# Latent attention with keys on partitions: three buffers for the rounded operands, value products in pairs, inverses by small transfers

## What is computed

```
s = (einsum('bhqd,bhkd->bhqk', q_nope, k_nope)
     + einsum('bhqr,bkr->bhqk', q_pe, k_pe)).astype(float32) * scale
p = softmax(s, axis=-1)
out = einsum('bhqk,bhkd->bhqd', p, v)
```

## Time and profile before

| | |
|---|---|
| median of three runs | 3343.63 us |
| profiled execution's own time | 3337.21 us |
| its span | 3335.4 us |
| TensorE matmuls busy | 3153.4 us (95%) |
| VectorE busy | 2228.0 us (67%) |
| ScalarE busy | 1356.4 us (41%) |
| mean granted TensorE clock | 0.976 of full |
| first and last exponential of the stage | 1970.2 and 2548.8 us from the span's start |

### The profile page before, as it was taken

One profiled execution on the slowest core, in us unless ns is written; L12 is line 12 of the kernel. 1 busy time (PEld: TensorE's weight loads), 2 busy tenths in 40 slices (PEclk: granted clock), 3 DMA queues, 4 the chain that ended last, 5 costly groups with the idle time before them and its releaser, 6 DMA issues. The chain is left out here.

```text
span 3335.4 us, 42351 instructions
## 1 busy us (share of the span) xinstructions
PE 3153.4 (95%) x16250; PEld 2516.4 (75%) x16250; DVE 2228.0 (67%) x2448; ACT 1356.4 (41%) x2259; POOL 571.6 (17%) x587
## 2 busy tenths in 40 slices
PE   7999899899999999999998989999999999999997
PEld 5888777788999999888886854444445878888875
DVE  4999666546755565778544347776776676667877
ACT  5121456465332333445674223333333433333444
POOL 0000000120222222332131100000000223332323
PEclk9999999899999999999999989999999999999998
DMA  6224685532212212667527523222221222222665
GB/s 213 70 95 150 207 262 202 173 113 73 75 61 76 70 61 70 233 216 239 176 81 287 173 69 63 56 56 56 65 55 52 100 64 84 87 83 76 236 209 196
DMA packets 302456, 415.52 MB, mean 125 GB/s; under 512 B 108840, under 2 KB 206824, under 8 KB 301232
## 3 DMA queue, kind: packets, MB, share of 16 engines
q1 hardware_dynamic: 288880, 363.12, 35.4%
q0 software_dynamic: 13376, 49.69, 4.0%
HBM read 318.49 MB, written 94.13 MB: 124 GB/s over the span
## 5 line engine op out<-in xcount | busy, mean ns | idle before, releaser
L4615 ACT ACTIVATE mla_e<-mla_scores 128x512 f32<-128x512 f32 x320 | 191.1, 597 | 391.0 <-PE mla_scores L90 383.3
L2160 DVE TENSOR_TENSOR ring_lo<-raw_rows,ring_hi 128x512 fp32r<-128x512 f32 x200 | 181.0, 905 | 202.3 <-ACT ring_hi L2011 202.0
L1283 PE MATMUL banks<-y_hi,ring_hi 128*128 128x384 f32 (+2 forms) x688 | 222.0, 323 | 4.2 <-DVEq L2148 3.7
L1285 PE MATMUL banks<-y_hi,ring_lo 128*128 128x384 f32 (+2 forms) x688 | 221.9, 322 | 0.0
L1284 PE MATMUL banks<-y_lo,ring_hi 128*128 128x384 f32 (+2 forms) x688 | 221.8, 322 | 0.0
L4645 DVE TENSOR_REDUCE mla_least<-mla_rounded 128x1 f32<-128x1024 f32 x128 | 153.1, 1214 | 86.6 <-PE mla_rounded L4534 86.4
L1283 PE MATMUL banks<-differences,ring_hi 128*128 128x512 f32 (+2 forms) x560 | 192.0, 343 | 3.4 <-ACT sums L2021 2.6
L1285 PE MATMUL banks<-differences,ring_lo 128*128 128x512 f32 (+2 forms) x560 | 191.8, 342 | 0.0
L1284 PE MATMUL banks<-differences,ring_hi 128*128 128x512 f32 (+2 forms) x560 | 191.8, 342 | 0.0
L862 DVE SCALAR_TENSOR_TENSOR ab_work<-ab_work,ab_taps 128x1295 f32<-128x1295 f32 x120 | 188.0, 1567 | 3.3
L4565 PE MATMUL mla_out<-mla_e,ckv 128*64 128x512 f32 x640 | 180.8, 645 | 0.0
(11 more groups left out here) (552 smaller groups left out, 8710.5 us busy)
## 6 DMA issues: line engine op xcount, KB each, us to landing
raw_rows<-in_ffn_w_up SPq DMA_DIRECT2D x88, 512.0 KB, 3.5
da_ada_w<-in_ada_w SPq DMA_DIRECT2D x10, 4096.0 KB, 14.5
raw_rows<-in_ffn_w_down SPq DMA_DIRECT2D x110, 256.0 KB, 3.1
raw_rows<-in_ffn_w_down SPq DMA_DIRECT2D x44, 512.0 KB, 4.7
out_raw<-scratch_act SPq DMA_DIRECT2D x66, 256.0 KB, 3.5
sums<-scratch_act SPq DMA_DIRECT2D x55, 256.0 KB, 3.4
ab_raw<-in_ab_w_in SPq DMA_DIRECT2D x20, 512.0 KB, 4.0
scratch_act<-conv_lines SPq DMA_DIRECT2D x20, 512.0 KB, 4.8
```

Of the source, the lines that this page charges most:

```text
L1283: pe.matmul(out, w_hi[:, w], b_hi[:, a:a + n], start=start and k == 0, stop=False, skip_group_check=True)
L1285: mm = pe.matmul(out, w_lo[:, w], b_hi[:, a:a + n], start=False, stop=k == KD // 2 - 1, skip_group_check=True)
L2160: dve.tensor_tensor(blocks(begun.lo(r)), source(r), blocks(begun.hi(r)).bitcast(F32), ALU.subtract)\
L4615: act.activation(e[:, tile % E_SLOTS, c * BANK:(c + 1) * BANK], s_ps[:, score_fill(h, i) % 3, :], ACT.Exp)\
```

## The change

- The rounded queries and keys get a third buffer (`q_hi`, `k_hi`, by h % 3); the rests keep two. SP loads the rounded parts of head h + 2 and the rests and values of head h + 1 at the start of head h. The pieces of the next head stand earlier (`piece_at`), the first behind block 0.
- The value products stand in pairs of key tiles, behind blocks 5, 9, 13 and 17, and the last pair behind block 1 of the next head. The sum stands behind block 5.
- VectorE adds all ten key tiles (nine adds), so the sum is one group of matmuls. There is one accumulator instead of two.
- ScalarE copies the sums to SBUF (`copy_sum`), SP turns them into a tile of 128 x 8 by eight transfers, VectorE takes the inverse of that, SP stores it to memory in one transfer and reads it back in two, spread over 64 partitions each. The last head keeps the old way.
- The rows of ones and zeros come from small tiles, by seven transfers, and the first loads of the stage come in another order.

The core of the diff (VectorE's order is in the rows above):

```diff
-    SUM_AT = 5
+    SUM_AT = 6
...
-    ADDS = KT - 2
+    ADDS = KT - 1
...
-    piece_at = {2: 0, 4: 1, 5: 2, 7: 3, 8: 4, 10: 5, 11: 6, 13: 7, 14: 8, 15: 9}
+    piece_at = {0: 0, 1: 1, 2: 2, 4: 3, 6: 4, 7: 5, 9: 6, 10: 7, 12: 8, 13: 9}
...
+        q_hi = q_first[0], sb("q_hi1", [HD + 1, SEQ], F32R), sb("q_hi2", [HD + 1, SEQ], F32R)
+        k_hi = k_first[0], sb("k_hi1", [HD + 1, T], F32R), sb("k_hi2", [HD + 1, T], F32R)
+        q_lo, k_lo = (q_first[1], sb("q_lo1", [HD + 1, SEQ], F32R)), (k_first[1], sb("k_lo1", [HD + 1, T], F32R))
...
+            def rounded(h):
+                if h >= 3:
+                    sp.wait_ge(s.s_full.sem, 2 * KT * (h - 2))
+                load_part(sp, h, q_hi[h % 3], k_hi[h % 3], q_parts[0], k_parts[0], hi_in[h % 3].sem)
+
+            def rests(h):
                 if h >= 2:
                     sp.wait_ge(s.s_full.sem, 2 * KT * (h - 1))
-                for part, signal in ((0, hi_in), (1, lo_in)):
-                    load_part(sp, h, part, qs[h % 2][part], ks[h % 2][part], q_parts, k_parts, signal[h % 2].sem)
+                load_part(sp, h, q_lo[h % 2], k_lo[h % 2], q_parts[1], k_parts[1], lo_in[h % 2].sem)
...
+            def sums_to_columns(h):
+                sp.wait_ge(s.sum_copied.sem, h + 1)
+                for t in range(XT):
+                    c, j = divmod(t, XT // 2)
+                    sp.dma_start(sum_cols[:, t:t + 1], sum_rows[c * C_V:c * C_V + 1, j * P:(j + 1) * P],
+                                 allow_slow_non_contiguous=True).then_inc(s.cols_in.sem, 16)
+
+            def store_inverses(h):
+                sp.wait_ge(s.inverted.sem, h + 1)
+                sp.dma_start(column(inv_rows[h % 2]), inv_cols[:, :], allow_slow_non_contiguous=True)\
+                  .then_inc(s.inv_stored.sem, 16)
+
+            def spread_inverses(h):
+                sp.wait_ge(s.inv_stored.sem, 16 * (h + 1))
+                sp.wait_ge(s.scaled.sem, h)
+                for c in range(2):
+                    sp.dma_start(inv[c * C_V:(c + 1) * C_V, :], row(inv_rows[h % 2, c * BANK:(c + 1) * BANK], C_V))\
+                      .then_inc(s.inv_in.sem, 16)
...
+            for n in (1, 2):
+                sp.dma_start(k_hi[n][C_NOPE:HD, :].bitcast(F32), k_parts[0][C_HEADS * C_NOPE:C_HEADS * C_NOPE + C_ROPE, :])\
+                  .then_inc(s.pe_in.sem, 16)
+            rounded(1)
+            sp.wait_ge(s.set.sem, 2)
+            for k in k_hi:
+                unit_row(k[HD:HD + 1, :], ones)
+            for k in k_lo:
+                unit_row(k[HD:HD + 1, :], zeros)
+            for q in q_lo:
+                unit_row(q[HD:HD + 1, :], zeros)
             values(0)
-            load_positions(sp, ks[1], k_parts, s.pe_in.sem)
-            head(1)
-            values(1)
             shift_row(0, 0)
             shift_row(0, 1)
+            sp.dma_start(k_lo[1][C_NOPE:HD, :].bitcast(F32), k_parts[1][C_HEADS * C_NOPE:C_HEADS * C_NOPE + C_ROPE, :])\
+              .then_inc(s.pe_in.sem, 16)
+            rests(1)
+            values(1)
+            rounded(2)
+            shift_row(1, 0)
+            shift_row(1, 1)
             for h in range(1, H):
-                if h >= 2:
-                    head(h)
-                    values(h)
-                shift_row(h, 0)
-                shift_row(h, 1)
+                if h + 1 < H:
+                    rests(h + 1)
+                    values(h + 1)
+                if h + 2 < H:
+                    rounded(h + 2)
+                sums_to_columns(h - 1)
+                store_inverses(h - 1)
+                if h + 1 < H:
+                    shift_row(h + 1, 0)
+                spread_inverses(h - 1)
+                if h + 1 < H:
+                    shift_row(h + 1, 1)
...
-                    tokens = slice(c * BANK, (c + 1) * BANK)
-                    pe.matmul(s_ps[c * C_V:(c + 1) * C_V, f % 3, :], ones[:, :], acc[:, h % 2, tokens],
-                              start=True, stop=False)
-                for c in range(2):
-                    tokens = slice(c * BANK, (c + 1) * BANK)
-                    mm = pe.matmul(s_ps[c * C_V:(c + 1) * C_V, f % 3, :], ones[:, :],
-                                   e[:, (h * KT + KT - 1) % E_SLOTS, tokens], start=False, stop=True)
+                    mm = pe.matmul(s_ps[c * C_V:(c + 1) * C_V, f % 3, :], ones[:, :], acc[:, c * BANK:(c + 1) * BANK],
+                                   start=True, stop=True)
                 mm.then_inc(s.sum_full.sem, 1)
...
                     if i == 1 and h:
+                        product(h - 1, KT - 2)
                         product(h - 1, KT - 1)
-                    if i >= 3 and i % 2:
+                    if i >= 5 and i % 4 == 1:
+                        product(h, (i - 5) // 2)
                         product(h, (i - 3) // 2)
                     if i == SUM_AT - 1 and h:
                         total(h - 1)
...
+            def copy_sum(h):
+                act.wait_ge(s.sum_full.sem, h + 1)
+                if h:
+                    act.wait_ge(s.cols_in.sem, 16 * XT * h)
+                act.activation(sum_rows[:, :], s_ps[:, sum_fill(h) % 3, :], ACT.Copy).then_inc(s.sum_copied.sem, 1)
...
-                    if i == 1 and h:
+                    if i == 2 and h:
                         copy_out(h - 1)
-                    if i == 9 and h and h % 2 == 0:
+                    if i == 6 and h:
+                        copy_sum(h - 1)
+                    if i == 18 and h and h % 2 == 0:
                         round_out(h // 2 - 1)
...
-                dve.wait_ge(s.sum_full.sem, h + 1)
-                dve.wait_ge(s.scaled.sem, h)
-                dve.reciprocal(inv, s_ps[:, sum_fill(h) % 3, :]).then_inc(s.inverted.sem, 1)
+                dve.wait_ge(s.cols_in.sem, 16 * XT * (h + 1))
+                if h:
+                    dve.wait_ge(s.inv_stored.sem, 16 * h)
+                dve.reciprocal(inv_cols[:, :], sum_cols[:, :]).then_inc(s.inverted.sem, 1)
+
+            def last_inverse():
+                dve.wait_ge(s.sum_full.sem, H)
+                dve.wait_ge(s.scaled.sem, H - 1)
+                dve.reciprocal(inv, s_ps[:, sum_fill(H - 1) % 3, :]).then_inc(s.inverted.sem, 1)
 
             def scale(h):
-                dve.wait_ge(s.inverted.sem, h + 1)
+                if h < H - 1:
+                    dve.wait_ge(s.inv_in.sem, 32 * (h + 1))
+                else:
+                    dve.wait_ge(s.inverted.sem, H)
```

More of the change, by code:

```diff
@@ L4434, in sb @@
             return ctx.enter_context(nc.sbuf_tensor(f"mla_{label}", shape, dt))
-        qs = q_first, [sb(f"q_{n}", [HD + 1, SEQ], F32R) for n in ("hi", "lo")]
-        ks = k_first, [sb(f"k_{n}", [HD + 1, T], F32R) for n in ("hi", "lo")]
+        ones = sb("ones", [P, C_V])
+        zeros = sb("zeros", [1, C_V])
+        least = sb("least", [P, 2, XT])
+        shift = sb("shift", [P, 2, XT], F32R)
+        q_hi = q_first[0], sb("q_hi1", [HD + 1, SEQ], F32R), sb("q_hi2", [HD + 1, SEQ], F32R)
+        k_hi = k_first[0], sb("k_hi1", [HD + 1, T], F32R), sb("k_hi2", [HD + 1, T], F32R)
+        q_lo, k_lo = (q_first[1], sb("q_lo1", [HD + 1, SEQ], F32R)), (k_first[1], sb("k_lo1", [HD + 1, T], F32R))
         v = v_home[:, 0, 0:2 * KT * C_V].rearrange("p (j k d) -> p j k d", j=2, k=KT)
@@ L4441, in latent_attention @@
         e = sb("e", [P, E_SLOTS, SEQ])
-        acc = sb("acc", [P, 2, SEQ])
-        ones = sb("ones", [P, C_V])
-        least = sb("least", [P, 2, XT])
-        shift = sb("shift", [P, 2, XT], F32R)
+        acc = sb("acc", [P, SEQ])
+        sum_rows = sb("sum_rows", [P, BANK])
+        sum_cols, inv_cols = sb("sum_cols", [P, XT]), sb("inv_cols", [P, XT])
         s_ps = ctx.enter_context(nc.psum_tensor("mla_scores", [P, 3, BANK], F32))
@@ new lines, in spread_inverses, with unit_row @@
+            def spread_inverses(h):
[4 more added lines that the diff above has]
+                      .then_inc(s.inv_in.sem, 16)
+            def unit_row(dst, value):
+                count = dst.shape[1] // C_V
+                sp.dma_start(dst.bitcast(F32).rearrange("p (a n) -> p a n", n=C_V),
+                             value[0:1, :].rearrange("p (a n) -> p a n", a=1).broadcast_to([1, count, C_V]))\
+                  .then_inc(s.unit_in.sem, 16)
@@ L4597, in _ @@
                         piece(h + 1, piece_at[i])
+            product(H - 1, KT - 2)
             product(H - 1, KT - 1)
@@ L4610, in exponential @@
                     act.wait_ge(s.o_step.sem, before + 1)
-                    if before % KT == KT - 1:
-                        act.wait_ge(s.sum_full.sem, before // KT + 1)
-                    else:
-                        act.wait_ge(s.added.sem, ADDS * (before // KT) + max(1, before % KT))
+                    act.wait_ge(s.added.sem, ADDS * (before // KT) + max(1, before % KT))
                 act.activation(e[:, tile % E_SLOTS, c * BANK:(c + 1) * BANK], s_ps[:, score_fill(h, i) % 3, :], ACT.Exp)\
@@ L4692, in _ @@
                 if h:
```

(31 more changed lines are left out.)

53 lines of the change are left out of this document (23 added, 30 removed).

## The result

The changed kernel took 3356.83 us (median of 6 runs, 3352.71 to 3360.73), the kernel before 3343.66 in the same session (6 runs, 3340.55 to 3346.26). The ratio is 1.004, interval 1.0027 to 1.0053: slower by 13 us, where I had put 3240 and left 0.04 for slower.

What follows compares the result with a forecast made beforehand. TensorE was taken to bound the attention stage, with holes and half clock. 14 heads from 37.16 to 30.5 us save 93.2, the start 13.4, the last head loses 2.4: 104.2 saved, forecast 3240 us, range 3220 to 3275.

Steps and rivals of the forecast that it cites:

- the walk: One attention head timed from its first score block through copy, columns, inverse, store, spread, scale and adds: 30.5 us a head.
- the spread: Reading the stored inverses back in two transfers of 128 KB: taken to land 2.5 us after issue.
- x = 2.0: Adds ending x us into the next head; beyond 2.0, a longer chain lengthens the head 1:1; x was 2.5.
- the reason for the low clock: The hole at each head's start, after which TensorE's clock was at 1.2 GHz; expected to go, leaving granted clock 1.00 mid-stage.
- the hole: TensorE's wait for the next head's rounded operands, 32.1 us over 14 heads; third buffers were to remove it.
- rival A: The transfers set the head: each leg 1 us longer, 33.5 us a head, total 3284; chance 0.12.
- Rival C: Slower than before: columns 7.2 and spread 3.0 us later in queues, 49 us slower, 3392; chance 0.04.
- threshold of 7 us of extra chain: In rival C, the extra chain per head from which the kernel turns slower: 104 / 15 = 7 us.
- TensorE's own work: TensorE's busy time in one attention head after the change: 29.8 us, from 32.7 before.
- The price of a pair: Two value products back to back on TensorE: 2.06 us, where a product alone costs 1.20.
- The start: Attention stage up to head 1's scores: reordered loads and earlier shift rows bring them to 1987.0 from 2000.4, 13.4 us saved.
- VectorE's sum: VectorE's work per head, reductions, adds, scale, half a residual and little ones: 25.5 of 29.8 us, so no bound.

Runs made afterwards that it cites:

- the run in which only the store differs: Changed kernel with the 4 KB store of the inverses as 128 runs of 32 bytes instead of 1024 single elements: 3229.13 us, ratio 0.9659.
- the runs with the later rounding: ScalarE's rounding moved from exponential 18 of an even head to 12 of the following odd head: changed kernel 3377.89 and 3383.02 us, 128-byte-run version 3222.41 us.
- the run with runs: Changed kernel with sums moved into a 32x32 tile by two transfers, inverted there and stored in 32 runs of 128 bytes: 3221.35 us, ratio 0.9636.

## Why the prediction was wrong

**The step that failed** is the price of one leg of the walk: "I take 4.2, the row nearest in shape", for the store of 1024 single elements. It measured 9.7. The row of 4.2 in the earlier trace rows has the same number of single elements, but they are loads; for stores of single elements there was no row. With 5.5 more there and 0.5 more in the spread the adds end 6.0 later, and by the walk's own rule (beyond x = 2.0 it goes 1:1 into the head) 30.5 becomes 36.5.

**A second term stood at nothing.** With 36.5 a head and 6.0 more in the last one the prediction's sum would still give 14 us faster. The kernel is 15 slower in the trace, so 30 us lie elsewhere: 18.5 in the 14 heads (37.82 for 36.5), 7.4 in the last, 3.7 at the start. The prediction let the reason for the low clock go with the hole and expected 1.00 in the middle of the stage. But TensorE's stalls come with the lower clock again, 0.90 over the 14 heads, and the walk has no term for it. Against the run in which only the store differs, a head is (529.45 - 418.50) / 14 = 7.9 us longer, where the walk gives 36.5 - 29.7 = 6.8. That the clock is the whole of the 30 is not shown; that ScalarE's block in front of the exponentials is part of it, the runs with the later rounding don't bear out. In the last head 6.0 of 13.4 are the chain, and TensorE stalls for 3.06 us in its first pair, behind ScalarE as in the head shown; the rest I have not divided up.

**The bounds failed with it.** I had bounded the store by 1.7 and 4.2, two rows of which neither is a store of single elements, and the 1 us a leg of rival A was no row's. Rival A named the mechanism, that the transfers set the head, and got 0.12 with 3284. Rival C, slower than before, had A's mechanism but put the extra in the columns and the spread, which landed in 2.0 and 3.0; it got 0.04. Its threshold of 7 us of extra chain was too high: with 6.0 the kernel is slower already. The Trainium skill's page DMA: Bandwidth & Descriptors (Rules for kernel authors) says that a non-contiguous last dimension becomes one descriptor for each element. The trace agrees: from 2203 to 2212, with the store and four shift rows of 128 elements out, 1536 elements, it counts 1616 packets. I had cited the rule and then priced the chain without it. The fixed cost of about 2.0 us that the prediction cites from the same page (Anatomy of one DMA) is given there for transfers that GpSimd issues; these are SP's, and the store in runs landed in 1.3.

**What held.** The holes for rounded operands went. TensorE's own work of 29.8 us a head, and 29.7 with a short store: 29.73 in the run with runs. The price of a pair: 2.06. Columns: 2.0 as taken, and in the head shown they land at 2202.95, 6.5 us after the copy's end at 2196.43 (predicted 19.4 - 13.2 = 6.2); VectorE's wait for them 0.84 there and 18.5 / 15 = 1.2 on average for "about 1 us". The order of the adds behind the scale, and that TensorE would stall at the reductions. The start gave 9.7 of 13.4; the stage began 1.5 later in this trace, as its first fill shows (the kernel before's row, then the changed one's), so 11.2. The scores began at 1958.7, before the 1962 that would have shown a late start:

```profile
1944.00 0.15 POOL L4720 MEMSET mla_ones<- 128x64 f32 x1 [28.11 <-POOLq L76]
...
1945.53 0.15 POOL L4785 MEMSET mla_ones<- 128x64 f32 x1 [28.11 <-POOLq L76]
```

One slip in VectorE's sum: nine adds of 1.31 are 11.8, not 11.5, so 25.8 of 29.8; nothing hangs on it.

**The whole sum, with a short store.** The run with runs ends its stage at 2443.00, 117.7 before 2560.66: 104.0 from 14 heads, 11.0 at the start, 2.6 at the end. With a store so short the prediction's terms give 14 x 7.46 + 13.4 = 118 and nothing lost at the end. The heads are right; that the whole is right is luck, since the start gave 2.4 less and the end, with shorter columns too, 2.6 more. By the medians this run gains 121, and the one in which only the store differs 114. The 3221.35 lies beside the 3225 that the prediction had for 29.7 a head.

## What to carry to other kernels

A round trip through memory on the critical chain is priced leg by leg, and each leg by its direction and its number of separate elements: a row with as many elements the other way (4.2 us here, against 9.7) is no bound. If such a chain makes TensorE stall, the slower clock after each stall is a term of its own. Lay a small tile out so that what is stored is runs (here 32 bytes were enough) even if the tile then has fewer partitions. And where a walk ends within 1 us of its slack, the case in which the sign turns deserves more than a few hundredths: ask which leg has no row at all.

## What the runs showed of the hardware

- A store of 4 KB from SBUF to memory landed after 1.3 us in 32 runs of 128 bytes, 1.4 in 128 runs of 32 bytes, 7.1 in 1024 single elements from 32 partitions, and 9.7 to 10.8 from 128 partitions. Between SBUF rows and columns 128 single elements took 2.0.
- In the last 3.6 us of such a store, and for 14.0 us with two of them out, the DMA engines show no work at all (share 0.00), so the profile's DMA share doesn't warn of it.
- Four small transfers issued right behind such a store on the same queue landed after 7.4 us; in the kernel before such transfers took 2.0.
- Two such stores issued together took 21.3 us until both had landed.
- Stalls of 63.4 us in 14 heads came with a mean granted clock of 0.90, and the same matmuls were busy for 466.0 us instead of 417.7 at 1.00.
- The landing of this store differs between chips or runs (medians 9.7, 10.5, 10.7 and 10.8 in four traces), that of the stores in runs did not (1.3 twice). So the changed kernel's time differs too, 3356.83 and 3375.11, while before stayed at 3343.66 and 3339.6.
